# Four moves in the order of two attention and recurrence layers: bank emptying before the rotary exchange, Fourier products split, scores and output pieces swapped

## The chip, the cores and the metric

The kernel runs on one core of a Trainium2 chip. The time is the device time of one execution, in microseconds (us), from three runs before the change. The trace and the page of the profile come from one further execution.

Five engines work side by side and wait for each other by semaphores: TensorE (PE; its weight loads have a row of their own, PEld), VectorE (DVE), ScalarE (ACT), GpSimd (POOL) and SyncE (SP). TensorE writes its products into eight PSUM banks; ScalarE and VectorE empty them.

## What is computed

The reference is two blocks on 256 tokens of width 1024. The first (adaptive norm, attention, pooling, 32 experts) is left as it is. The second has two layers, and the change is in them:

```python
def second_block(x, positions, attn_norm_w, w_in, hgrn_lower_bounds, w_out, mlp_norm_w, w_up, w_down, final_norm_w):
    ...
    for layer in range(DEPTH_2):
        h = rms_norm_2(x, attn_norm_w[layer])
        proj = h @ w_in[layer]
        a_q, a_i, a_zf, a_zb, a_g, b_u, c_q, c_k, c_v = jnp.split(proj, SPLIT_POINTS, axis=-1)
        o_a = hgrn2_mixer(a_q, a_i, a_zf, a_zb, a_g, lb_all[layer]).astype(x.dtype)
        o_b = fourier_mixer(b_u).astype(x.dtype)
        o_c = dilated_attention_mixer(c_q, c_k, c_v, positions).astype(x.dtype)
        mixed = jnp.concatenate([o_a, o_b, o_c], axis=-1)
        x = x + mixed @ w_out[layer]
        h = rms_norm_2(x, mlp_norm_w[layer])
        x = x + jnp.square(jax.nn.relu(h @ w_up[layer])) @ w_down[layer]
    return rms_norm_2(x, final_norm_w)
```

`hgrn2_mixer` is a gated recurrence in two directions with 4 heads, `fourier_mixer` a 2-D Fourier transform of 256 columns, and `dilated_attention_mixer` an attention of 8 heads, with rotary positions on q and k. All data are float32.

## The kernel before

Every engine has one program, written out by hand in the order in which it runs: `pe_layer`, `dve_layer` and `act_layer` are called once for each layer (l = 0, 1). No scheduler moves anything. An engine that waits holds up all that stands behind it in its own program.

TensorE takes banks in a fixed rotation (`g.take`): all eight in turn, and in the attention part the first four only, while banks 4 to 7 hold the four output pieces. `take` waits until the bank's last content was read. `g.evac(e, key)` waits until that key's bank was read, `g.full` until it was written.

A layer runs on TensorE in this order. *Projections* of 256 columns each (L541, L553) fill banks "in" and "av". Between them stand the pieces of the recurrence:

- `pe_hgrn(l, dr, c)` for direction dr and half c. With c = 0 it first fills two **large** banks, "far" (L1125, L1131). Then it fills, for each of two token halves, two banks "lv" with 56 small products (L1146). VectorE prepares their inputs in `dve_decay` (last instruction L2278), and takes the results off in `dve_pairs` (L2295, L2297), which stands ahead of the decay of the next direction. The far banks are read by ScalarE in `act_far` (L1566, L1567, two of each). The last "lv" pair of direction 0 comes eight banks after the far pair, and so reuses its banks.
- `pe_hgrn_out` (L1171, L1173) multiplies what the pairs gave with the values. It waits for two copies by ScalarE (L1456, semaphore `placed`).
- the Fourier products "V" (L989) over channels, four of them, two for each 128 columns c, read by ScalarE at L1469; and four products each for "four" (L1004) over tokens, read at L1477.
- "os" (L993), the sum of squares of the recurrence's output.

The rotary exchange is `act_turn_halves`: ScalarE issues four DMAs (L1527) that swap halves of q (or k). VectorE multiplies and adds them (L2070, L2071, L2074); the third sum (`rot_ready` 3) admits the scores of head pairs 0 and 1, the fourth those of pairs 2 and 3.

The attention works on four head pairs c = 0 to 3 (heads 2c and 2c+1). `pe_layer_scores(c)` (L1186) makes two banks of scores; `pe_layer_turn(c)` (L1199) transposes the probabilities of its two heads; `pe_layer_mix(c)` (L1212) multiplies them with v; `pe_out_first` (L1231) is one of four output pieces of 16 matmul records, over the first half of `mix`, and depends on no head. VectorE's order for the heads is a loop:

```python
    for h in range(2, 8):
        dve_layer_score(e, g, l, h)
        if h > 2:
            dve_layer_prob(e, g, l, h - 1)
    dve_layer_prob(e, g, l, 7)
```

`dve_layer_score` reads a score bank (L2218) and finds the maxima (L2220); ScalarE exponentiates (L1536); `dve_layer_prob` divides by the sum (L2226, L2230) and raises `prob_ready`, for which the transposes of that head wait. After the attention comes the rest of the output (L1030), and the up and down projections, where TensorE works without a pause.

Of the kernel before, what the change touches and what calls it, by code (L numbers as in the profile page):

```python
# [10 lines left out]
P = 128  # L11
D = 1024
S = 256
KC = D // P
ST = S // P
# [516 lines left out]
def h_ready(e, g, n, k):  # L532
    e.wait_ge(g.s["h_shifted" if n < 2 else "h_scaled"], KC * n + k + 1)
# [410 lines left out]
def pe_layer(e, g, l):  # L944
    s = g.s
    n = 2 + 2 * l
    ready = lambda k: h_ready(e, g, n, k)
    raw = lambda which: lambda k: e.wait_ge(s["xw"], KC * (2 * l + which) + k + 1)

    def project(tile, oc):  # L950
        w = g.filled(e, layer_tile(l, tile))
        for jj in range(2):
            pe_chunk(e, g, ("in", l, oc + jj), w, jj, 256, KC, g.h, ready)
        g.owed += 1

    def tokens(tile, j):
        w = g.filled(e, layer_tile(l, tile))
        pe_tokens(e, g, ("av", l, j), w, g.h, ready)
        g.owed += 1

    for tile in range(2):
        w = g.filled(e, layer_tile(l, tile))
        for jj in range(2):
            pe_chunk(e, g, ("in", l, 4 + 2 * tile + jj), w, jj, 256, KC, g.xw, raw(0))
            if tile == jj == 0 and l:
                pe_norm_added(e, g, n)
            if tile == 0 and jj == 1 and l == 0:
                pe_norm_two(e, g)
        g.owed += 1
    project(2, 0)  # L970
    tokens(3, 0)
    project(4, 10)
    project(5, 12)
    pe_hgrn(e, g, l, 0, 0)
    pe_hgrn(e, g, l, 0, 1)
    project(6, 14)
    project(7, 16)
    project(8, 2)
    pe_hgrn(e, g, l, 1, 0)
    project(9, 8)  # L980
    pe_hgrn(e, g, l, 1, 1)
    tokens(10, 1)
    pe_hgrn_out(e, g, l)
    for c in range(2):
        for tt in range(ST):
            u = g.take(e, ("V", l, c, tt))
            e.wait_ge(s["late_in"], 16)
            g.evac(e, "in", l, 8 + c)
            g.last(u, e.matmul(u.ap[:, 0:S], g.uT[:, c, tt * P:(tt + 1) * P], g.c("dft_c"), start=True, stop=True))  # L989
    u = g.take(e, ("os", l))  # L990
    e.wait_ge(s["o_square"], 2 * l + 2)
    for c in range(2):
        ins = e.matmul(u.ap[:, c * S:(c + 1) * S], g.c("headones"), g.tmp4[:, c, :], start=True, stop=True)  # L993
    g.last(u, ins)
    pe_layer_scores(e, g, l, 0)
    tokens(11, 2)
    for c in range(2):
        u = g.take(e, ("four", l, c))
        e.wait_ge(s["late_in"], 16)
        for tt in range(ST):  # L1000
            g.evac(e, "V", l, c, tt)
        for n4 in range(4):
            part, tt = n4 // 2, n4 % 2
            ins = e.matmul(u.ap[:, 0:S], g.V[:, tt, c, part * P:(part + 1) * P], g.c("dft_t", (part * ST + tt) * S, S), start=n4 == 0, stop=n4 == 3)  # L1004
        g.last(u, ins)

    g.cycle, g.turn = range(4), 0
    out = []
    pe_layer_scores(e, g, l, 1)
    pe_layer_turn(e, g, l, 0)  # L1010
    pe_layer_scores(e, g, l, 2)
    pe_out_first(e, g, l, out)
    pe_layer_turn(e, g, l, 1)
    pe_layer_mix(e, g, l, 0)
    pe_layer_scores(e, g, l, 3)
    pe_out_first(e, g, l, out)
    pe_layer_turn(e, g, l, 2)
    pe_layer_mix(e, g, l, 1)
    pe_out_first(e, g, l, out)
    pe_layer_turn(e, g, l, 3)  # L1020
    pe_layer_mix(e, g, l, 2)
    pe_out_first(e, g, l, out)
    pe_layer_mix(e, g, l, 3)
    g.cycle, g.turn = range(8), 0
    for j in range(4):
        w = g.filled(e, layer_tile(l, 12 + j))
        for jj in range(2):
            for k in range(4, KC):
                g.evac(e, "m", l, k - 4)
                ins = e.matmul(out[j].ap[:, jj * S:(jj + 1) * S], w[:, k * 256 + jj * P:k * 256 + (jj + 1) * P], g.mix[:, k, :],  # L1030
                               start=False, stop=k == KC - 1, skip_group_check=True)
                if k < KC - 1:
                    g.hand_back(ins)
        g.last(out[j], ins)
        g.owed += 1

    for j in range(2):
        w = g.filled(e, layer_tile(l, 16 + j))
        for jj in range(2):
            oc = 2 * j + jj  # L1040
            pe_chunk(e, g, ("up", l, oc), w, jj, 256, KC, g.xw, raw(1))
            if oc == 0:
                pe_norm_added(e, g, n + 1)
        g.owed += 1
    for i in range(SEVENS):
        pe_seven(e, g, l, i)
    w = g.filled(e, layer_tile(l, 18 + SEVENS))
    e.wait_ge(s["hid_ready"], UPS * (l + 1))
    for jj in range(2):
        pe_chunk(e, g, ("down", l, jj), w, jj, 256, KC, g.hid[:, 24:32, :], lambda k: None)  # L1050
    g.owed += 1
# [102 lines left out]
def pe_hgrn_out(e, g, l):  # L1154
    for dr in range(2):
        for j in range(2):
            g.evac(e, "far", l, dr, j)
    e.wait_ge(g.s["far_out"], 4 * (l + 1))
    e.wait_ge(g.s["placed"], 2 * (l + 1))
    g.evac(e, "av", l, 0, 1)  # L1160
    for c in range(2):
        u = g.take(e, ("o", l, c))
        for tt in range(ST):
            for far in range(2):
                for j in range(2):
                    lo, hd = DH * j, 2 * c + j
                    v = slice(hd * DH, (hd + 1) * DH)
                    q = u.ap[lo:lo + DH, tt * P:(tt + 1) * P]
                    if far:
                        al = 4 * (1 - tt) + 2 * j + c  # L1170
                        ins = e.matmul(q, g.av[:, 1 - tt, v], g.AL[:, al * P:(al + 1) * P], start=False, stop=True)  # L1171
                    else:
                        ins = e.matmul(q, g.av[:, tt, v], g.AT[:, hd, tt * P:(tt + 1) * P], start=True, stop=False)  # L1173
                    if tt == far == 1 and j == 0:
                        ins.then_inc(g.s["o_half"], 1)
        g.last(u, ins)


def pe_layer_scores(e, g, l, c):

    us = [g.take(e, ("s", l, 2 * c + j)) for j in range(2)]
    e.wait_ge(g.s["rot_ready"], 4 * l + 3 + c // 2)
    for qt in range(ST):
        for j in range(2):
            lo = DH * j
            ins = e.matmul(us[j].ap[:, qt * S:(qt + 1) * S], g.cq[lo:lo + DH, c, qt * P:(qt + 1) * P], g.ck[lo:lo + DH, c, :],  # L1186
                           start=True, stop=True)
            if qt == 1:
                g.last(us[j], ins)


def pe_layer_turn(e, g, l, c):
    for j in range(2):
        h = 2 * c + j
        u = g.take(e, ("t", l, h))
        e.wait_ge(g.s["prob_ready"], 8 * l + h + 1)
        for kt in range(ST):
            for qt in range(ST):
                ins = e.transpose(u.ap[:, (2 * kt + qt) * P:(2 * kt + qt + 1) * P], g.prob[h % 4][:, qt * S + kt * P:qt * S + (kt + 1) * P],  # L1199
                                  g.c("ident"))  # L1200
        g.last(u, ins)


def pe_layer_mix(e, g, l, c):
    u = g.take(e, ("m", l, c))
    for j in range(2):
        g.evac(e, "t", l, 2 * c + j)
    g.evac(e, "av", l, 2, 1)
    for kt in range(ST):
        for j in range(2):  # L1210
            lo, h = DH * j, 2 * c + j
            ins = e.matmul(u.ap[lo:lo + DH, 0:S], g.cv[:, kt, h * DH:(h + 1) * DH], g.prob_t[h % 4][:, kt * S:(kt + 1) * S],  # L1212
                           start=kt == 0, stop=kt == 1)
            if kt == 1 and j == 0:
                ins.then_inc(g.s["mix_half"], 1)
    g.last(u, ins)


def pe_out_first(e, g, l, out):


    j = len(out)
    w = g.filled(e, layer_tile(l, 12 + j))
    u = g.take(e, ("lout", l, j), 4 + j)
    for jj in range(2):
        for k in range(4):
            if k < 2:
                e.wait_ge(g.s["hg_ready"], l + 1)
            else:
                g.evac(e, "four", l, k - 2)  # L1230
            e.matmul(u.ap[:, jj * S:(jj + 1) * S], w[:, k * 256 + jj * P:k * 256 + (jj + 1) * P], g.mix[:, k, :],  # L1231
                     start=k == jj == 0, stop=False, skip_group_check=True)
    out.append(u)
# [160 lines left out]
def act_layer(e, g, l):  # L1394
    s = g.s
# [40 lines left out]
            tokens(0)  # L1436
    for oc in range(10, 14):
        evict(oc)
    act_turn_halves(e, g, l, 0)
    act_far(e, g, l, 0)  # L1440
    for lv in range(NL):
        act_decay(e, g, l, 1, lv)
        if lv % 2 == 0:
# [1011 lines left out]
```

## Time and profile before

| what | value |
|---|---|
| median of 3 runs | 1407.7 us (1407.31 to 1408.53) |
| profiled execution, its time | 1408.37 us |
| profiled execution, its span | 1406.6 us, so 1.77 us lie around the span |
| TensorE busy | 1380.7 us |
| VectorE, ScalarE busy | 661.8 us, 264.2 us |
| granted TensorE clock, mean | 0.996 of full |

The span is from the first to the last instruction. Busy time of TensorE is the time in which a matmul is in flight; what is left of the span are its pauses. A row of the timeline gives in brackets how long the engine was idle before it and what ended that. "issue" is a pause for which the profile names no partner.

### The profile page before, as it was taken

Reading aid. Unit: us, or ns where it says so; the run is one execution under the profiler, and the core shown is the slowest. Engines: PE = TensorE matmul, PEld = TensorE weight load, DVE = VectorE, ACT = ScalarE, POOL = GpSimd, SP = SyncE. Lnnn points to the kernel's source line nnn. Section 1 sums busy time; section 2 is a strip of 40 time slices with the busy share of each in tenths; the row PEclk is TensorE's granted clock in tenths of the full one; section 3 lists DMA queues with packets and bytes.
Section 4 is the critical chain, followed back from the end, with each engine's and each line's share of the span. In section 5 each row is a group of like instructions: output and inputs, shape, how many; then the busy total and the mean of one; then the engine's idle time right before and its main releaser. Section 6 shows DMA issues by size and latency. Waiting matters only on the chain.

```text
span 1406.6 us, 22243 instructions
## 1 busy us (share of the span) xinstructions
PE 1380.7 (98%) x9402; PEld 1061.7 (75%) x9402; DVE 661.8 (47%) x1483; ACT 264.2 (19%) x565; POOL 4.0 (0%) x10
## 2 busy tenths in 40 slices
PE   9999999999999999999999999999999999999997
PEld 6888887454445544554488789999998878999997
DVE  2467554111111111111278837775445883777544
ACT  2234201100000000000243431220014343122000
POOL 0000000000000000000000000000000000000000
PEclk9999999999999999999999999999999999999999
DMA  9995656999999999999944224444544413444420
GB/s 392 354 398 197 265 215 274 422 422 420 420 420 422 420 421 420 423 421 421 418 166 132 83 101 171 178 161 169 181 150 150 151 61 124 171 158 179 165 76 31
DMA packets 51237, 362.95 MB, mean 258 GB/s; under 512 B 6064, under 2 KB 6384, under 8 KB 7872
## 3 DMA queue, kind: packets, MB, share of 16 engines
q1 hardware_dynamic: 48528, 353.39, 63.4%
q10 hardware_dynamic: 2032, 5.96, 1.4%
q0 software_dynamic: 576, 2.14, 0.4%
q8 instruction: 77, 1.26, 0.4%
q14 instruction: 24, 0.20, 0.0%
HBM read 358.31 MB, written 1.06 MB: 255 GB/s over the span
## 4 chain that ended last, share of the span: by engine, by line
PE 92%; DMA 2%; DVE 2%; ACT 1%; issue 1%; ACTq 0%; DVEq 0%; SPq 0%
PE bank L1094 26%; PE bank L839 22%; PE bank L541 19%; PE bank L553 4%; PE bank L827 4%; PE bank L849 4%; DMA ring<-in_weights 2%; PE bank L1231 2%; PE bank L658 2%; PE bank L1030 2%; PE bank L1186 1%; PE bank L1212 1%; PE bank L613 1%; PE bank L1146 1%; PE bank L1199 1%
## 5 line engine op out<-in xcount | busy, mean ns | idle before, releaser
L541 PE MATMUL bank<-h,ring 128*128 128x256 f32 x832 | 185.6, 383 | 0.8 <-issue 0.7
L541 PEld LDWEIGHTS bank<-h,ring 128*128 128x128 f32 x832 | 158.0, 191 | 23.8 <-issue 2.3
L839 PE MATMUL bank<-ring,x_s 128*64 128x512 f32 x768 | 167.8, 592 | 1.4 <-issue 0.9
L839 PEld LDWEIGHTS bank<-ring,x_s 128*64 128x64 f32 x768 | 56.1, 137 | 109.9 <-issue 109.9
L1094 PE MATMUL bank<-hid,ring 128*128 128x128 f32 x912 | 115.6, 275 | 0.0
L1094 PE MATMUL bank<-h,ring 128*128 128x128 f32 x896 | 113.8, 275 | 0.0
L1094 PEld LDWEIGHTS bank<-hid,ring 128*128 128x128 f32 x912 | 108.6, 192 | 0.0
L1094 PEld LDWEIGHTS bank<-h,ring 128*128 128x128 f32 x896 | 107.0, 192 | 0.1
L1936 DVE TENSOR_TENSOR act<-act,bank 128x512 f32<-128x512 f32 x16 | 11.0, 688 | 195.5 <-PE bank L839 195.5
L1094 PE MATMUL bank<-sq,ring 128*128 128x128 f32 x720 | 95.1, 275 | 0.0
L1094 PEld LDWEIGHTS bank<-sq,ring 128*128 128x128 f32 x720 | 87.6, 192 | 0.0
L839 PE MATMUL bank<-ring,a_s 128*64 128x512 f32 x384 | 85.0, 595 | 0.0
L553 PE MATMUL bank<-ring,h 128*128 128x256 f32 x320 | 71.2, 381 | 0.0
L1094 PE MATMUL bank<-ring 128*128 128x128 f32 x512 | 67.6, 275 | 0.0
L553 PEld LDWEIGHTS bank<-ring,h 128*128 128x128 f32 x320 | 60.2, 190 | 9.3 <-issue 1.3
L1919 DVE TENSOR_TENSOR x_s<-bank,mod 128x512 f32<-128x512 f32 x32 | 22.1, 692 | 95.7 <-PE bank L827 95.7
L839 PEld LDWEIGHTS bank<-ring,a_s 128*64 128x64 f32 x384 | 26.5, 137 | 49.4 <-issue 48.0
L1094 PEld LDWEIGHTS bank<-ring 128*128 128x128 f32 x512 | 62.3, 192 | 0.0
L849 PEld LDWEIGHTS bank<-put,gy 128*128 128x128 f32 x256 | 47.3, 190 | 19.8 <-issue 14.0
L827 PE MATMUL bank<-pick,h 128*128 128x128 f32 x512 | 61.4, 279 | 0.7 <-DVE pick L1911 0.7
L827 PEld LDWEIGHTS bank<-pick,h 128*128 128x128 f32 x512 | 59.9, 196 | 0.8 <-issue 0.8
L849 PE MATMUL bank<-put,gy 128*128 128x256 f32 x256 | 59.5, 385 | 1.0 <-DVE gy L1943 1.0
(353 smaller groups left out, 1734.7 us busy)
## 6 DMA issues: line engine op xcount, KB each, us to landing
ring<-in_weights SPq DMA_DIRECT2D x288, 1024.0 KB, 12.4
ringx<-in_weights SPq DMA_DIRECT2D x48, 1024.0 KB, 19.6
x<-in_x SPq DMA_DIRECT2D x1, 1024.0 KB, 5.1
pool_a<-in_cst ACTq DMA_DIRECT2D x1, 1024.0 KB, 6.2
bias<-bias_rows POOLq DMA_DIRECT2D x1, 1024.0 KB, 16.9
ring<-cq ACTq DMA_DIRECT2D x8, 128.0 KB
ring<-ck ACTq DMA_DIRECT2D x8, 128.0 KB, 2.4
out<-h ACTq DMA_DIRECT2D x2, 512.0 KB, 3.6
```

The source lines that it names most:

```text
L541: ins = e.matmul(u.ap[:, 0:S], w[:, k * width + j * P:k * width + (j + 1) * P], acts[:, k, :], start=k == 0, stop=k == kc - 1)
L553: ins = e.matmul(u.ap[:, 0:256], acts[:, k, tt * P:(tt + 1) * P], w[:, k * 256:(k + 1) * 256], start=k == 0, stop=k == KC - 1)
L613: ins = e.matmul(u.ap[32 * q:32 * q + 32, 0:256], g.spread[:, k, :], w[:, k * 256:(k + 1) * 256], start=m == 0, stop=m == 1)
L658: ins = e.matmul(u.ap[:, 0:S], w[:, k * 256 + jj * P:k * 256 + (jj + 1) * P], g.h[:, k, :], start=k == 0, stop=k == KC - 1)
L827: ins = e.matmul(g.bank[bank + k // 4][:, (k % 4) * P:(k % 4 + 1) * P], g.h_tok[:, tt, k * P:(k + 1) * P], g.pick[:, tt * P:(tt + 1) * P], ...
L839: ins = e.matmul(g.bank[bank][ex * SLOTS:(ex + 1) * SLOTS, :], stat(m)[:, ex * SLOTS:(ex + 1) * SLOTS], pair[ex][:, m * 512:(m + 1) * 512] ...
L849: ins = e.matmul(g.bank[4 + oc // 2][:, (oc % 2) * S:(oc % 2 + 1) * S], gy[:, oc * P:(oc + 1) * P], put[:, :], start=p == oc % 2 == 0, sto ...
L1030: ins = e.matmul(out[j].ap[:, jj * S:(jj + 1) * S], w[:, k * 256 + jj * P:k * 256 + (jj + 1) * P], g.mix[:, k, :], start=False, stop=k == ...
L1094: ins = e.matmul(u.ap[:, at * P:(at + 1) * P], a[:, k, :], act[:, k, :], start=k == 0 and (of == 1 or (b == 0 and first)), stop=k == 3 and ...
L1146: ins = e.matmul(us[j].ap[HB * b:HB * b + HB, lv * HB:(lv + 1) * HB], k, q, start=True, stop=True)
L1231: e.matmul(u.ap[:, jj * S:(jj + 1) * S], w[:, k * 256 + jj * P:k * 256 + (jj + 1) * P], g.mix[:, k, :], start=k == jj == 0, stop=False, sk ...
L1919: e.tensor_tensor(g.x_s[:, 512 * half:512 * half + 512].rearrange("p (k t) -> p k t", k=4), g.bank[bank + half][:, :].rearrange("p (k t) - ...
```

## The change

Three parts of a layer's order are written otherwise; no instruction is added or removed. `pe_channels` is a new function with the body of the old loop, for one c.

```diff
@@ -980,13 +980,9 @@
     project(9, 8)
     pe_hgrn(e, g, l, 1, 1)
     tokens(10, 1)
+    pe_channels(e, g, l, 0)
     pe_hgrn_out(e, g, l)
-    for c in range(2):
-        for tt in range(ST):
-            u = g.take(e, ("V", l, c, tt))
-            e.wait_ge(s["late_in"], 16)
-            g.evac(e, "in", l, 8 + c)
-            g.last(u, e.matmul(u.ap[:, 0:S], g.uT[:, c, tt * P:(tt + 1) * P], g.c("dft_c"), start=True, stop=True))
+    pe_channels(e, g, l, 1)
     u = g.take(e, ("os", l))
     e.wait_ge(s["o_square"], 2 * l + 2)
     for c in range(2):
@@ -1008,12 +1004,12 @@
     out = []
     pe_layer_scores(e, g, l, 1)
     pe_layer_turn(e, g, l, 0)
+    pe_out_first(e, g, l, out)
     pe_layer_scores(e, g, l, 2)
-    pe_out_first(e, g, l, out)
     pe_layer_turn(e, g, l, 1)
     pe_layer_mix(e, g, l, 0)
+    pe_out_first(e, g, l, out)
     pe_layer_scores(e, g, l, 3)
-    pe_out_first(e, g, l, out)
     pe_layer_turn(e, g, l, 2)
     pe_layer_mix(e, g, l, 1)
     pe_out_first(e, g, l, out)
...
@@ -1436,8 +1441,8 @@
             tokens(0)
     for oc in range(10, 14):
         evict(oc)
+    act_far(e, g, l, 0)
     act_turn_halves(e, g, l, 0)
-    act_far(e, g, l, 0)
```

The line numbers shift by a few. TensorE in the attention of the first layer, before: L1199 is a turn, L1186 scores, L1231 an output piece, L1212 a mix.

```order
L1199 MATMUL bank<-cst,hm 128x128 [waits prob_ready,bank_free_2]
...
L1199 MATMUL bank<-cst,hm 128x128 [waits prob_ready,bank_free_3]
...
L1186 MATMUL bank<-ck,cq 128x256 [waits rot_ready,bank_free_1,bank_free_0]
L1186 MATMUL bank<-ck,cq 128x256 x3
L1231 MATMUL bank<-mixed,ring 128x256 [waits hg_ready,bank_free_4,slot_filled_4]
...
L1231 MATMUL bank<-mixed,ring 128x256 [waits bank_free_6]
...
L1199 MATMUL bank<-cst,hm 128x128 [waits prob_ready,bank_free_2]
...
L1199 MATMUL bank<-cst,hm 128x128 [waits prob_ready,bank_free_3]
...
L1212 MATMUL bank<-hm,cv 64x256 [waits bank_free_3,bank_free_5,bank_free_2,bank_free_0]
```

The same place in the changed kernel (turn L1204, scores L1191, output piece L1236, mix L1217):

```order
L1204 MATMUL bank<-cst,hm 128x128 [waits prob_ready,bank_free_2]
...
L1204 MATMUL bank<-cst,hm 128x128 [waits prob_ready,bank_free_3]
...
L1236 MATMUL bank<-mixed,ring 128x256 [waits hg_ready,bank_free_4,slot_filled_4]
...
L1236 MATMUL bank<-mixed,ring 128x256 [waits bank_free_6]
...
L1191 MATMUL bank<-ck,cq 128x256 [waits rot_ready,bank_free_1,bank_free_0]
L1191 MATMUL bank<-ck,cq 128x256 x3
L1204 MATMUL bank<-cst,hm 128x128 [waits prob_ready,bank_free_2]
...
L1204 MATMUL bank<-cst,hm 128x128 [waits prob_ready,bank_free_3]
...
L1217 MATMUL bank<-hm,cv 64x256 [waits bank_free_3,bank_free_5,bank_free_2,bank_free_0]
```

The output piece and the scores of pair 2 have changed places, so that the turn of pair 1 stands right behind the scores of pair 2. Output piece 1 and the scores of pair 3, further down, change in the same way. The banks stay the same.

TensorE at the chunk outputs of the first layer, before (L1173 waits for `placed`, L989 are the Fourier products):

```order
L1173 MATMUL bank<-sq_106,av 64x128 [waits far_out,placed,bank_free_6,bank_free_0,bank_free_5,bank_free_3]
...
L1171 MATMUL bank<-hal,av 64x128 x2
...
L1173 MATMUL bank<-sq_106,av 64x128 [waits bank_free_4]
...
L989 MATMUL bank<-cst,uT 128x256 [waits bank_free_3,late_in,bank_free_5]
L989 MATMUL bank<-cst,uT 128x256 [waits bank_free_3,late_in,bank_free_6]
L989 MATMUL bank<-cst,uT 128x256 [waits bank_free_4,late_in,bank_free_7]
L989 MATMUL bank<-cst,uT 128x256 [waits bank_free_4,late_in,bank_free_0]
```

The same in the changed kernel (L1169 waits for `placed`, L1181 are the Fourier products):

```order
L1181 MATMUL bank<-cst,uT 128x256 [waits bank_free_3,late_in]
L1181 MATMUL bank<-cst,uT 128x256 [waits bank_free_3,late_in,bank_free_4]
L1169 MATMUL bank<-sq_106,av 64x128 [waits far_out,placed,bank_free_6,bank_free_0,bank_free_5]
...
L1167 MATMUL bank<-hal,av 64x128 x2
...
L1169 MATMUL bank<-sq_106,av 64x128 [waits bank_free_6]
...
L1181 MATMUL bank<-cst,uT 128x256 [waits bank_free_4,late_in,bank_free_7]
L1181 MATMUL bank<-cst,uT 128x256 [waits bank_free_4,late_in,bank_free_0]
```

Two of the four Fourier products now stand ahead of the wait for `placed`, in banks 3 and 4.

ScalarE behind the copies of q in the first layer, before: L1527 are the four DMA issues of the rotary exchange, L1566 and L1567 empty the far banks.

```order
L1418 COPY cq<-bank 128x256 [waits bank_full_4]
L1527 DMA ring<-cq 32x1024 [waits bank_free_3,bank_free_4,bank_free_2,bank_free_1]
L1527 DMA ring<-cq 32x1024 x3
L1566 COPY hal<-bank 128x256 [waits bank_full_5]
L1567 COPY sq_106<-bank 64x2x2x64
L1566 COPY hal<-bank 128x256 [waits bank_full_6]
L1567 COPY sq_106<-bank 64x2x2x64
L1558 ACTIVATE mixed<-mixed 128x512 [waits ex_in]
```

And in the changed kernel (L1532 are the issues, L1571 and L1572 empty the far banks):

```order
L1423 COPY cq<-bank 128x256 [waits bank_full_4]
L1571 COPY hal<-bank 128x256 [waits bank_full_5]
L1572 COPY sq_106<-bank 64x2x2x64
L1571 COPY hal<-bank 128x256 [waits bank_full_6]
L1572 COPY sq_106<-bank 64x2x2x64
L1532 DMA ring<-cq 32x1024 [waits bank_free_3,bank_free_4,bank_free_2,bank_free_1]
L1532 DMA ring<-cq 32x1024 x3
L1563 ACTIVATE mixed<-mixed 128x512 [waits ex_in]
```

The four copies stand ahead of the four issues.

## Rows read from the trace of the kernel before

**Rows 1.** The profile's page, busy time of TensorE, its share and instructions.

```profile
PE 1380.7 (98%) x9402; PEld 1061.7 (75%) x9402; DVE 661.8 (47%) x1483; ACT 264.2 (19%) x565; POOL 4.0 (0%) x10
```

**Rows 2.** TensorE's timeline, first layer, attention: start, duration, line, tiles, [idle before].

```profile
804.62 1.09 PE L1199 MATMUL bank<-cst,hm 128*128 128x128 f32 x8
806.84 1.13 PE L1186 MATMUL bank<-ck,cq 64*128 64x256 f32 x8 [1.12 <-issue]
807.90 3.72 PE L1231 MATMUL bank<-mixed,ring 128*128 128x256 f32 x16
811.46 1.04 PE L1199 MATMUL bank<-cst,hm 128*128 128x128 f32 x8
812.43 1.08 PE L1212 MATMUL bank<-hm,cv 128*64 128x256 f32 x8
813.44 1.13 PE L1186 MATMUL bank<-ck,cq 64*128 64x256 f32 x8
```

**Rows 3.** VectorE's timeline in the same stretch of the first layer.

```profile
802.25 0.69 DVE L2087 TENSOR_TENSOR mixed<-sg,gs 128x512 f32<-128x512 f32 x1
...
806.05 0.68 DVE L2218 SCALAR_TENSOR_TENSOR hm<-bank,cst 128x512 f32<-128x512 f32 x1
...
808.10 0.68 DVE L2218 SCALAR_TENSOR_TENSOR hm<-bank,cst 128x512 f32<-128x512 f32 x1
...
809.42 0.15 DVE L2226 RECIPROCAL small<-small 128x2 f32<-128x2 f32 x1
809.61 0.62 DVE L2230 TENSOR_SCALAR hm<-hm,small 128x256 f32<-128x256 f32 x2
...
814.68 0.69 DVE L2218 SCALAR_TENSOR_TENSOR hm<-bank,cst 128x512 f32<-128x512 f32 x1 [2.41 <-PE bank L1186]
```

**Rows 4.** ScalarE's timeline there: the second Fourier bank is emptied.

```profile
803.67 0.37 ACT L1477 COPY mixed<-bank 128x256 f32<-128x256 f32 x1 [1.36 <-PE bank L1004]
```

**Rows 5.** TensorE's timeline, blocks L1146 and L1125, both layers.

```profile
745.41 0.93 PE L1146 MATMUL bank<-hm 64*64 64x64 f32 x48 [0.70 <-ACT sq L1567]
...
767.65 0.71 PE L1125 MATMUL bank<-hm 64*128 64x128 f32 x8
...
1093.54 0.81 PE L1146 MATMUL bank<-hm 64*64 64x64 f32 x38 [0.70 <-ACT sq L1567]
1095.37 0.39 PE L1146 MATMUL bank<-hm 64*64 64x64 f32 x10 [1.03 <-issue]
...
1116.72 0.71 PE L1125 MATMUL bank<-hm 64*128 64x128 f32 x8
```

**Rows 6.** VectorE's timeline, last row of the second decay, both layers.

```profile
767.16 0.42 DVE L2278 TENSOR_TENSOR hm<-mixed,kk 128x256 f32<-128x256 f32 x1
...
1115.39 0.42 DVE L2278 TENSOR_TENSOR hm<-mixed,kk 128x256 f32<-128x256 f32 x1
```

**Rows 7.** ScalarE's timeline, second layer: rotary exchange issued, last large bank emptied.

```profile
1089.72 2.46 ACTq L1527 DMA_DIRECT2D ring<-cq  x4
...
1093.01 0.38 ACT L1567 COPY sq<-bank 64x256 f32<-64x256 f32 x1
```

**Rows 8.** DMA queues from 1093.00 to 1093.25 us: packets, MB, share of 16 engines.

```profile
q10 hardware_dynamic: 13, 0.05, 98.8%
q8 instruction: 1, 0.02, 23.6%
```

**Rows 9.** TensorE's timeline, first layer: chunk outputs, Fourier products, first scores.

```profile
787.24 0.44 PE L1173 MATMUL bank<-sq,av 128*64 128x128 f32 x4 [0.63 <-ACT sq L1456]
...
789.14 2.00 PE L989 MATMUL bank<-cst,uT 128*128 128x256 f32 x8
...
791.93 1.13 PE L1186 MATMUL bank<-ck,cq 64*128 64x256 f32 x8
```

**Rows 10.** ScalarE's copies into `AT` (first), VectorE's third rotary sum, first layer.

```profile
785.63 1.26 ACT L1456 COPY sq<-sq 64x512 f32<-64x512 f32 x2 [7.50 <-DVE sq L2063]
...
790.90 0.69 DVE L2074 TENSOR_TENSOR ck<-ck,ring 128x512 f32<-128x512 f32 x1
```

More of the change, by code:

```diff
@@ L1176, in pe_hgrn_out, with pe_channels @@
         g.last(u, ins)
+def pe_channels(e, g, l, c):
+    for tt in range(ST):
+        u = g.take(e, ("V", l, c, tt))
+        e.wait_ge(g.s["late_in"], 16)
+        g.evac(e, "in", l, 8 + c)
+        g.last(u, e.matmul(u.ap[:, 0:S], g.uT[:, c, tt * P:(tt + 1) * P], g.c("dft_c"), start=True, stop=True))
 def pe_layer_scores(e, g, l, c):
```

## The prediction

> **What bounds the kernel now.** I read the page first, for the share of TensorE. It is busy for 1380.7 us [rows 1] of a span of 1406.6, so a new order can gain no more than its 25.9 us of pauses, and any new pause is added in full, as nothing behind it waits for anything but TensorE. Then I read TensorE's timeline in both layers for the pauses at the three places that change. They are few: 1.12 us ahead of the scores of pair 2 [rows 2], 0.70 us ahead of the last L1146 block and, in the second layer, 1.03 us inside it [rows 5], and 0.63 us ahead of the chunk outputs [rows 9]. Last I read VectorE and ScalarE at the same moments, for what each pause waited for and what comes due right behind it. These rows decide the sum: a pause that is removed is worth only what lies between it and the next due time. The attention part has the same shape in both layers, so I work it out once and take it twice. All sums are made for the profiled execution (1408.37 us, its span and 1.77 us around it); it lies 0.67 us above the median of 1407.7, and I carry the difference to the median.
>
> **Attention, what is removed.** From the first turn (804.62) to the scores of pair 2 (806.84) pass 2.22 us [rows 2]. A turn with nothing in its way passes in 811.46 to 812.43, 0.97 us. So the pause costs 1.25 us at the pace of starts. The profile calls it "issue", but the scores need the two banks that VectorE is still reading: its second L2218 ends at 806.05 + 0.68 = 806.73 [rows 3] and the scores start at 806.84, 0.11 us later. In the new order output piece 0 stands here. What it needs is there: `hg_ready` at 802.25 + 0.69 = 802.94 [rows 3] and the second "four" bank at 803.67 + 0.37 = 804.04 [rows 4], against 805.59, when the turn is over. The piece passes in 807.90 to 811.46, 3.56 us [rows 2], longer than the pause. The 1.25 us go.
>
> **Attention, what is added.** The turn of pair 1 now stands right behind the scores of pair 2. Its second head, 3, needs `dve_layer_prob(3)`, and that stands in VectorE's loop behind `dve_layer_score(4)`, which needs the scores that TensorE has only just made. Before, the output piece lay over this round trip. Now it is bare. I work it out from the start S of the scores:
>
> - VectorE begins the score of the new pair at S + 1.24, as at 813.44 and 814.68, where it did wait for them [rows 2, 3].
> - From that to the division of the head before it pass 809.42 − 808.10 = 1.32 us, and the division ends 0.81 us later (809.61 + 0.62 − 809.42) [rows 3]. That is S + 3.37.
> - TensorE starts 0.11 us later, by the 806.73 and 806.84 above: S + 3.48.
> - TensorE itself is there after the scores (806.84 to 807.90, 1.06 us [rows 2]) and the transposes of the first head (half of 0.97, 0.49): S + 1.55.
>
> The new pause is 1.93 us, and it occurs twice in a layer, with scores 2 and scores 3. Behind the waiting transposes stand the mix, the next output piece and the next scores, so VectorE and ScalarE get everything later too, and the second pause is not filled by the first. The third and fourth turn have output pieces ahead of them as before. Sum for a layer: 2 × 1.93 − 1.25 = +2.61 us, for two +5.2 us. The least sure number is 0.11 us for waking TensorE. Behind ScalarE's copies into `AT`, which end at 785.63 + 1.26 = 786.89, TensorE started at 787.24, 0.35 us later [rows 9, 10]. With that in all four places the sum is 5.2 + 4 × 0.24 = +6.2 us. I take 0.11, as it is VectorE that wakes TensorE in both places.
>
> **The large banks.** ScalarE spends 2.46 us on four DMA issues ahead of the copies, and the last copy ends at 1093.01 + 0.38 = 1093.39 [rows 7]; the block starts at 1093.54 [rows 5]. TensorE has filled the far pair before the three L1146 blocks that precede this one, so copies that stand ahead of the issues start up to 2.46 us sooner, and the 0.70 us wait goes in both layers. What is due next is the next L1125, which needs VectorE's whole second decay. In the first layer the decay ends at 767.16 + 0.42 = 767.58 [rows 6] and TensorE is there at 767.65 [rows 5]. TensorE cannot come any earlier: worth 0. In the second it ends at 1115.39 + 0.42 = 1115.81 [rows 6], TensorE is there at 1116.72 [rows 5], and with 0.11 to wake it 0.80 us are to be had at most. VectorE's chain up to there has no gap that this edit shortens, as it still has the decay to do that stands behind the pairs.
>
> Whether the 0.80 are reached hangs on the 1.03 us inside the block [rows 5]. No engine released it. In the quarter microsecond from 1093.00 the instruction queue q8 began one packet, while the rotary exchange on q10 filled the DMA engines to 98.8% [rows 8]. I read the 1.03 us as instructions that had not yet arrived. Then they arrive at their own time, and TensorE, started earlier, waits longer there. The exchange now begins more than a microsecond later, which may let the packet through sooner. Bounds 0 and 0.80; I take 0.4 us, for the second layer alone. The later exchange itself costs nothing: the first layer's rotary sums end at 791.59 [rows 10], 46 us behind the block of 745.41 [rows 5].
>
> The Trainium skill ("Runtime: NRT & Kernel Launch", Instruction fetch mechanics) says that instructions are fetched in blocks of 256 and that crossing from one block to the next is mostly hidden. By that rule the 1.03 us would be no fetch, and the 0.80 us would be gained whole, which makes the sum 0.4 us smaller. The trace speaks against it with the 1.03 us beside the q8 packet.
>
> **The Fourier products.** Two of the four (half of the 2.00 us of eight records [rows 9]) now run while TensorE waited 0.63 us for ScalarE. They cover the wait. But behind them comes the first scores at 791.93 [rows 9], which need the third rotary sum; VectorE has it at 790.90 + 0.69 = 791.59 [rows 10]. With 0.11 us to wake, 791.70: of the 0.63 us no more than 0.23 remain, and with 0.35 to wake nothing. I take 0.1 for each layer, 0.2 us in all, bounds 0 and 0.46. VectorE's own chain is not shortened by this edit.
>
> **Sum.** +5.2 − 0.4 − 0.2 = +4.6 us: 1408.37 becomes 1413.0, the median 1407.7 becomes 1412.3. By the bounds: least 5.2 − 0.80 − 0.46 = +3.9, most +6.2, so 1411.6 to 1413.9.
>
> **Rivals.** 0.2% of the time, 2.8 us, is about what a measurement of this kernel can tell from no change.
>
> - *Both early edits pay in full, the attention costs what I say.* The pauses at the large banks (2 × 0.70 + 1.03) and at the chunk outputs (2 × 0.63) are 3.7 us. Then 5.2 − 3.7 = +1.5 us, 1409.2. It needs VectorE to be off the path in between; the two pairs 767.58 / 767.65 and 791.59 / 791.93 speak against it.
> - *Faster: the round trip is not bare.* If the probabilities of head 3 were there by S + 1.55, the two swaps would only remove 1.25 us each, and with my 0.6 the kernel would gain 3.1 us: 1404.6. It decides at a round trip of 1.55 us against my 3.48; VectorE's two scans and division alone take 2.13 of it, so little speaks for it. It would need the loop to stand otherwise.
> - *The cost is larger.* The attention at its upper bound, and one more instruction gap of 1.03 us in each layer, since blocks of instructions now end in other places against the waits: 6.2 + 2.1 = +8.3, less what the early edits give (0.6): 1415.4. For it speaks the 1.03 us itself; against it that no other such gap shows in the stretches I read.
> - *Attention as forecast, the early edits worth nothing:* inside my range, 1412.9.
>
> **How the numbers follow.** My forecast has 72 in 100, the full early gains 12, the larger cost 11, the faster case 5. The predicted time is that of the likeliest, 1412.3. Its own range is 1411.6 to 1413.9. The range over all cases goes down to 1410.0, which takes in partial gains of the first rival, and up to 1414.6, half way to the larger cost. Faster by over 0.2% (below 1404.9): 0.04. Within 0.2% (to 1410.5): 0.14. Slower: 0.82.
>
> **What would show it.** In the new trace the scores of pair 2 have no pause ahead of them, and the transposes of heads 3 and 5 each start after about 1.9 us of pause, released by L2230's counterpart on VectorE; the stretch from the first turn to the rest of the output (L1030) is 2.6 us longer in each layer. If these pauses are under 1 us, the step "round trip bare" is wrong. ScalarE's last far copy ends ahead of the last L1146 block, and that block starts without a wait; the next L1125 starts at the end of VectorE's decay in both layers. If it starts later in the second, the instructions were late. Ahead of the chunk outputs there is no pause, and there is one of about half a microsecond ahead of the first scores. The prediction is wrong as a whole if the time lies at or below 1410, which would mean that the early edits moved VectorE's chain too.

## The result, and the profile after

The changed kernel takes 1420.09 us (six runs, 1415.14 to 1421.34) where the kernel before takes 1408.05 (six runs, 1407.21 to 1408.53): a ratio of 1.0081, interval 1.0067 to 1.0095. It is slower, as forecast, but by 12.0 us and not by 4.6. Two executions of one later kernel, `swap_half_filled`, took 1451.86 and 1797.84 us at a mean granted clock of 0.944 and 0.752 and are left out of its times. The profiled execution of the changed kernel took 1419.98 us:

```profile
span 1418.1 us, 22243 instructions
...
PE 1386.2 (98%) x9402; PEld 1063.5 (75%) x9402; DVE 661.9 (47%) x1483; ACT 263.3 (19%) x565; POOL 4.1 (0%) x10
```

The span has grown by 11.5 us, TensorE's busy time by 5.5 [rows 1], though it has the same 9402 matmul records (a float32 product leaves two). So a good part of the loss is not a pause: the same work took longer. TensorE's timeline in the attention of the first layer answers to [rows 2] (turn L1204, scores L1191, output piece L1236, mix L1217, rest of the output L1026):

```profile
804.37 1.09 PE L1204 MATMUL bank<-cst,hm 128*128 128x128 f32 x8
805.30 3.62 PE L1236 MATMUL bank<-mixed,ring 128*128 128x256 f32 x16
808.85 1.14 PE L1191 MATMUL bank<-ck,cq 64*128 64x256 f32 x8
809.91 0.66 PE L1204 MATMUL bank<-cst,hm 128*128 128x128 f32 x4
812.36 0.63 PE L1204 MATMUL bank<-cst,hm 128*128 128x128 f32 x4 [1.79 <-DVE hm L2235]
812.92 1.82 PE L1217 MATMUL bank<-hm,cv 128*64 128x256 f32 x8
814.67 4.63 PE L1236 MATMUL bank<-mixed,ring 128*128 128x256 f32 x16
819.23 1.14 PE L1191 MATMUL bank<-ck,cq 64*128 64x256 f32 x8
...
822.74 0.62 PE L1204 MATMUL bank<-cst,hm 128*128 128x128 f32 x4 [1.79 <-DVE hm L2235]
823.30 1.95 PE L1217 MATMUL bank<-hm,cv 128*64 128x256 f32 x8
825.17 4.50 PE L1236 MATMUL bank<-mixed,ring 128*128 128x256 f32 x16
829.51 1.04 PE L1204 MATMUL bank<-cst,hm 128*128 128x128 f32 x8
...
836.15 4.15 PE L1026 MATMUL bank<-mixed,ring 128*128 128x256 f32 x18
```

The pause ahead of the scores is gone. The turn of pair 1 stops after its first head, and the second starts at 812.36 after 1.79 us, released by VectorE's L2235 (before: L2230), and the same at 822.74. But look at what follows. The first mix passes in 812.92 to 814.67, 1.75 us, where it took 1.01 before (812.43 to 813.44 [rows 2]); the output piece takes 4.56 us (814.67 to 819.23) and not 3.56. The windows show why (the columns are the stretch, its length, and the busy time and, in brackets, the instructions of PE, PEld, DVE, ACT and POOL; then PEclk, the granted clock, 1.00 being full, the DMA share and GB/s):

```profile
812.90:814.70 1.80, 1.80 (x10) 0.72 (x9) 1.32 (x4) 1.13 (x5) 0.00 (x0) 0.56 0.00 0
814.70:819.20 4.50, 4.50 (x18) 3.57 (x16) 0.00 (x0) 1.19 (x3) 0.00 (x0) 0.80 0.00 0
...
823.30:825.20 1.90, 1.90 (x10) 0.78 (x9) 1.43 (x5) 1.25 (x5) 0.00 (x0) 0.52 0.04 9
825.20:829.50 4.30, 4.30 (x18) 3.67 (x17) 0.66 (x3) 1.07 (x3) 0.00 (x0) 0.82 0.00 2
829.50:836.10 6.60, 6.60 (x41) 4.73 (x39) 0.00 (x0) 1.45 (x3) 0.00 (x0) 1.00 0.00 0
```

Right behind each of these pauses the granted clock is near half, the lower of its levels (1.2 GHz); over the output piece it averages 0.80 and 0.82, and in the last window it is back at the full 2.4 GHz. From the first turn to the rest of the output pass 836.15 − 804.37 = 31.78 us; before it was

```profile
804.62:830.25 25.63, 24.51 (x147) 18.89 (x145) 12.11 (x30) 12.29 (x36) 0.00 (x0) 1.00 0.00 1
```

The 6.15 us more are two pauses at the pace of starts, 809.91 to 812.36 less the 0.49 of one head, 1.96 us each, less the 1.25 removed: 2.67 us. The other 3.5 us are the work behind them at the lower clock: 0.74 and 1.00 behind the first pause, 0.86 and 0.78 behind the second (mix 823.30 to 825.17, output piece 825.17 to 829.51), and 0.07 for each second head. The second layer is alike, 1191.26 − 1159.53 = 31.73 us where 25.62 passed, so both layers together lose 12.3 us: 5.3 of pauses and 7.0 behind them.

That TensorE's busy time grew by 5.5 us and not by 7.0 comes for the most part from a place that the change does not touch. In the first block stand three pauses of 0.70, 0.99 and 0.73 us within some five microseconds, in both profiled executions. Behind them the clock fell in that of the kernel before and not in that of the changed kernel. The first row and window are of the kernel before, the second ones of the changed kernel:

```profile
107.12 8.83 PE L541 MATMUL bank<-h,ring 128*128 128x256 f32 x32 [0.73 <-issue]
107.12:115.79 8.67, 8.67 (x32) 7.34 (x33) 5.83 (x20) 4.38 (x12) 0.00 (x0) 0.80 0.09 35
...
107.09 7.15 PE L541 MATMUL bank<-h,ring 128*128 128x256 f32 x32 [0.73 <-issue]
107.09:114.07 6.98, 6.98 (x33) 6.17 (x33) 4.25 (x17) 2.71 (x10) 0.00 (x0) 1.00 0.11 43
```

The same 32 records take 1.7 us more where the clock averages 0.80. VectorE's side of the pause, answering to [rows 3]:

```profile
810.08 0.69 DVE L2223 SCALAR_TENSOR_TENSOR hm<-bank,cst 128x512 f32<-128x512 f32 x1 [2.16 <-PE bank L1191]
...
811.60 0.62 DVE L2235 TENSOR_SCALAR hm<-hm,small 128x256 f32<-128x256 f32 x2
```

The score waits 2.16 us for TensorE, starts 1.23 us after the scores (808.85), and the division ends at 812.22, 0.14 us before the transposes start. This is the round trip as I had it.

The early edits, in the block of [rows 5] and at the places of [rows 9]:

```profile
746.39 0.34 PE L1142 MATMUL bank<-aq,kk 64*64 64x64 f32 x7 [1.29 <-issue]
746.67 3.50 PE L541 MATMUL bank<-h,ring 128*128 128x256 f32 x15
```

```profile
1101.39 0.39 PE L1142 MATMUL bank<-hm 64*64 64x64 f32 x10 [2.07 <-issue]
```

```profile
787.34 0.44 PE L1169 MATMUL bank<-sq,av 128*64 128x128 f32 x4
...
791.67 1.14 PE L1191 MATMUL bank<-ck,cq 64*128 64x256 f32 x8 [0.21 <-DVE ck L2079]
```

ScalarE's wait of 0.70 us is gone, and one pause ("issue") of 1.29 us stands in its place in the first layer, of 2.07 us in the second, where 1.03 stood. The projection starts at 746.67. The next L1121 (before: L1125) starts at 767.59 and 1122.74 us, 0.39 and 1.02 us behind the end of VectorE's decay (767.20 and 1121.72). Ahead of the chunk outputs (787.34) is no pause, and there is one of 0.21 ahead of the first scores.

### The profile page after: what moved, and what is told of

It is laid out like the page before. It is cut to its first block, busy times and chain, and to the rows that moved or that the text cites. A ratio compares the mean times of both kernels' runs of the same rounds, so it can differ in the third digit from the quotient of the medians.

```text
span 1418.1 us, 22243 instructions
## 1 busy us (share of the span) xinstructions
PE 1386.2 (98%) x9402; PEld 1063.5 (75%) x9402; DVE 661.9 (47%) x1483; ACT 263.3 (19%) x565; POOL 4.1 (0%) x10
## 3 DMA queue, kind: packets, MB, share of 16 engines
q8 instruction: 77, 1.26, 0.3%
## 4 chain that ended last, share of the span: by engine, by line
PE 91%; DVE 4%; DMA 2%; issue 1%; ACT 1%; DVEq 0%; SPq 0%; ACTq 0%
PE bank L1090 26%; PE bank L839 22%; PE bank L541 18%; PE bank L553 4%; PE bank L827 4%; PE bank L849 4%; DMA ring<-in_weights 2%; PE bank L1236 2%; PE bank L658 2%; PE bank L1026 2%; PE bank L1142 1%; PE bank L1217 1%; PE bank L1191 1%; PE bank L613 1%; PE bank L1000 0%
## 5 line engine op out<-in xcount | busy, mean ns | idle before, releaser
L541 PE MATMUL bank<-h,ring 128*128 128x256 f32 x832 | 183.9, 381 | 1.3 <-issue 1.2
L541 PEld LDWEIGHTS bank<-h,ring 128*128 128x128 f32 x832 | 157.3, 190 | 23.4 <-issue 2.7
```

What stands on the lines that cost most here:

```text
L541: ins = e.matmul(u.ap[:, 0:S], w[:, k * width + j * P:k * width + (j + 1) * P], acts[:, k, :], start=k == 0, stop=k == kc - 1)
```

## Experiments

Each is compared with the kernel before on the same chip. There the kernel before had medians of 1407.46, 1409.23, 1408.94 and 1408.88 us, and its executions spread from 1405.9 to 1410.9. The ratio compares the executions of one round with each other, and each difference in us below is worked out from the ratio (0.1% is 1.4 us), not from the medians.

**The exchange alone, and the early edits alone.** `swap_only` has only this:

```diff
     pe_layer_turn(e, g, l, 0)
+    pe_out_first(e, g, l, out)
     pe_layer_scores(e, g, l, 2)
-    pe_out_first(e, g, l, out)
     pe_layer_turn(e, g, l, 1)
     pe_layer_mix(e, g, l, 0)
+    pe_out_first(e, g, l, out)
     pe_layer_scores(e, g, l, 3)
-    pe_out_first(e, g, l, out)
```

> Only the scores and output pieces change places. Theory 1 (the pauses ahead of heads 3 and 5 cost 2.7 us a layer, and TensorE's clock falls to half behind each of them, another 3.5 us a layer): +12.3 us, 1420.3 against 1408.0, with the granted clock near 0.5 right behind each 1.8 us pause. Theory 2 (the early edits have a part in the loss): clearly less, +5 to +9 us.

Measured: 1420.49 us, ratio 1.0087 (1.0070 to 1.0103), +12.2 us. The exchange alone makes a loss of the same size as the whole change. `early_only` has the other two parts of the diff and not this one.

> Only ScalarE's copies ahead of the rotary exchange and the Fourier split; the attention as before. Theory 1: what these edits remove is due again right behind, so -0.2 to -1.0 us, and no loss. Theory 2 (they cost something): +3 to +7 us.

Measured: 1409.29 us, ratio 1.0005 (0.9993 to 1.0017). That is no loss of the size of theory 2. A gain isn't shown either; the interval reaches from −1.0 to +2.4 us. The trace shows what can eat the gain. It is of an execution of 1410.26 us, and in its second layer stand:

```profile
1096.13 0.39 PE L1142 MATMUL bank<-hm 64*64 64x64 f32 x10 [1.79 <-issue]
```

```profile
1098.00:1100.00 2.00, 2.00 (x6) 1.58 (x5) 1.97 (x4) 0.00 (x0) 0.00 (x0) 0.50 0.69 229
```

Where I had hoped for a gain of 0.4 us stands a pause of 1.79 us, and behind it the clock is at half: 6 matmul records in 2 us, where the kernel before has 11. In the first layer of the same execution the pause is 1.64 us and the clock stays full.

**Pause or clock.** Is it TensorE's standing still that slows the work behind it, or VectorE and ScalarE reading banks beside it? `swap_filled` is the changed kernel with work in the pause:

```diff
         u = g.take(e, ("t", l, h))
+        if j and c in (1, 2):
+            for i in range(4):
+                e.matmul(u.ap[:, 0:S], g.c("ident"), g.c("dft_t", 0, S), start=True, stop=True)
         e.wait_ge(g.s["prob_ready"], 8 * l + h + 1)
```

> The changed kernel, with four products of 128x256 that nobody reads put into the bank of the second head ahead of its wait, in the turns of pairs 1 and 2: 1.73 us of work inside a pause of 1.96 us at the pace of starts. Extra work is done, the wait for the head stays. Theory 1 (the clock falls because TensorE stands still): the clock stays at 1.0 and the mix and output piece behind take 1.01 and 3.56 us as before the change; the time is before + 5.3 - 0.9, about 1412.5, some 7 us faster than the changed kernel. Theory 2 (mix and output piece are slow because VectorE and ScalarE read banks beside them): no faster than the changed kernel, 1420.

Measured: 1412.63 us, ratio 1.0034 (1.0022 to 1.0046), +4.8 us. It does more work than the changed kernel and is about 7 us faster. The trace is of an execution of 1416.37 us, one of the slower ones, as the clock fell elsewhere in it (behind a pause of 1.72 us in the small-product block of the first layer). L1203 are the unread products, L1207, L1220 and L1239 turn, mix and output piece:

```profile
813.51 1.89 PE L1203 MATMUL bank<-cst 128*128 128x256 f32 x8
815.38 0.66 PE L1207 MATMUL bank<-cst,hm 128*128 128x128 f32 x4
815.96 1.08 PE L1220 MATMUL bank<-hm,cv 128*64 128x256 f32 x8
816.98 3.72 PE L1239 MATMUL bank<-mixed,ring 128*128 128x256 f32 x16
820.63 1.14 PE L1191 MATMUL bank<-ck,cq 64*128 64x256 f32 x8
```

```profile
815.96:816.98 1.02, 1.02 (x10) 0.49 (x9) 0.98 (x3) 0.30 (x1) 0.00 (x0) 1.00 0.00 0
816.98:820.63 3.65, 3.65 (x19) 2.96 (x17) 0.38 (x2) 2.01 (x7) 0.00 (x0) 1.00 0.00 0
```

The second head still starts 2.36 us behind the first (813.02 to 815.38), so nearly all of the round trip is still there (2.45 us in the changed kernel). The mix takes 1.02 us and the output piece 3.65, at full clock, and so in all four places of the two layers. The stretch from the first turn to the rest of the output takes 28.39 us (807.47 to 835.86), 2.8 more than before; the prediction has 2.6.

`swap_half_filled` has two such products in place of four.

> The changed kernel with two unread products in the waits of heads 3 and 5 in place of four, so that TensorE stands still for about 0.9 us there and not 1.79. Theory 1 (a pause as long as 1.8 us lets the clock fall; the 1.12 us ahead of scores 2 in the kernel before did not): clock 1.0 behind it, time as with four products, 1412 to 1413. Theory 2 (any pause at this place with little work around it does it): the falls stay, 1416 to 1420.

```profile
815.47 0.66 PE L1207 MATMUL bank<-cst,hm 128*128 128x128 f32 x4 [0.84 <-DVE hm L2238]
```

```profile
816.00:820.00 4.00, 4.00 (x24) 3.08 (x23) 1.38 (x5) 2.32 (x7) 0.00 (x0) 1.00 0.00 0
```

With 0.84 us left to stand still the clock holds, in all four places. Two executions count, 1414.63 and 1416.32 us, too few for an interval. The rows bear theory 1 out, the time does not confirm it: the profiled execution, 1416.32, had a fall elsewhere, behind a pause of 2.00 us in the small-product block of the first layer.

**One exchange.** `swap_one` moves only output piece 0 ahead of scores 2:

```diff
     pe_layer_turn(e, g, l, 0)
+    pe_out_first(e, g, l, out)
     pe_layer_scores(e, g, l, 2)
-    pe_out_first(e, g, l, out)
     pe_layer_turn(e, g, l, 1)
```

> The kernel before with only the first of the two exchanges: output piece 0 ahead of scores 2; scores 3 stay ahead of output piece 1. Theory 1: one round trip of 1.96 us at the pace of starts is bare and one fall of the clock follows, the 1.25 us ahead of scores 2 go: +0.7 + 1.75 = +2.5 us a layer, +5 us in all. Theory 2 (the loss of the exchanges is joint, one alone is free or gains): -2.5 to +1 us.

Measured: 1413.41 us, ratio 1.0033 (1.0020 to 1.0045), +4.7 us. One exchange costs by itself, so the loss is not a joint effect of the two. But they do not cost the same. In the trace the stretch is longer by 2.6 us in the first layer and 2.7 in the second, where both exchanges cost 6.1: each has its pause of 1.96 us and its fall, and the 1.25 us that the change removes are credited to the first alone.

```profile
811.89 0.63 PE L1199 MATMUL bank<-cst,hm 128*128 128x128 f32 x4 [1.80 <-DVE hm L2230]
```

```profile
814.00:816.00 2.00, 1.63 (x8) 1.15 (x8) 0.00 (x0) 1.42 (x5) 0.00 (x0) 0.51 0.00 0
816.00:820.00 4.00, 4.00 (x21) 3.21 (x20) 3.35 (x8) 1.09 (x4) 0.00 (x0) 1.00 0.00 0
```

**The cause of the round trip.** `swap_dve` is the changed kernel with another order on VectorE:

```diff
     for h in range(2, 8):
         dve_layer_score(e, g, l, h)
-        if h > 2:
-            dve_layer_prob(e, g, l, h - 1)
-    dve_layer_prob(e, g, l, 7)
+        if h % 2:
+            dve_layer_prob(e, g, l, h - 1)
+            dve_layer_prob(e, g, l, h)
```

> The changed kernel, with VectorE dividing heads 2 and 3 ahead of score 4, and heads 4 and 5 ahead of score 6. Theory 1 (the pause is the round trip through score h+1 that VectorE's loop puts ahead of the division): the pauses ahead of heads 3 and 5 go, and with them the clock's falls; what is left is the gain, 2 x 1.25 for the pause ahead of scores 2 and some 0.6 of the early edits: 1404.9. Theory 2 (the division is late for another reason, as ScalarE's exponentials): pauses of 1 us or more stay.

Measured: 1405.75 us, ratio 0.9986 (0.9976 to 0.9996), faster than the kernel before. The first turn, the turn of pair 1 and the rest of the output:

```profile
804.54 1.09 PE L1204 MATMUL bank<-cst,hm 128*128 128x128 f32 x8
...
810.08 1.10 PE L1204 MATMUL bank<-cst,hm 128*128 128x128 f32 x8
...
829.08 11.28 PE L1026 MATMUL bank<-mixed,ring 128*128 128x256 f32 x51
```

```profile
808.53 0.17 DVE L2231 RECIPROCAL small<-small 128x2 f32<-128x2 f32 x1 [0.44 <-ACT hm L1541]
808.73 0.62 DVE L2235 TENSOR_SCALAR hm<-hm,small 128x256 f32<-128x256 f32 x2
810.25 0.69 DVE L2223 SCALAR_TENSOR_TENSOR hm<-bank,cst 128x512 f32<-128x512 f32 x1 [0.90 <-PE bank L1191]
```

Head 3 is divided at 808.73 to 809.35, ahead of score 4 at 810.25, and the turn at 810.08 runs through. The stretch takes 24.54 us where 25.63 passed, 1.1 less. `swap_dve_only` is this exchange and this order without the early edits.

> The exchange of scores and output pieces with VectorE's divisions moved ahead of the next scores, ScalarE and the Fourier products as before. Theory 1 (the early edits give little or nothing, as their pause is due again): the 1.1 us a layer that the attention lost by its pause are gained, 1405.2 to 1405.8 where before is 1407.5. Theory 2 (the early edits gave a good part of the 1.7 us): half of that gain or less, 1406.5 or more.

Measured: 1406.87 us, ratio 0.9986 (0.9976 to 0.9995), the same ratio as with them, and each is known to 0.1%. Theory 1 held, also in that no gain of the early edits shows.

**The pause in the small-product block.** I had read it as the wait for the next block of instructions. `early_shifted` is `early_only` with products that nobody reads in the routing part, 128 instructions:

```diff
         ins = e.matmul(u.ap[:, 0:512], g.xs[:, 0, 0:P], g.xs[:, 0:2, :], start=True, stop=True)
+    for i in range(32):
+        ins = e.matmul(u.ap[0:64, 0:64], g.xs[:, 0, 0:64], g.xs[:, 0, 0:64], start=True, stop=True)
     g.last(u, ins)
```

> Only the two early edits, and 32 products of 64x64 that nobody reads, 128 instructions of TensorE, put into the routing part some 500 us ahead. Theory 1 (the pause in the last small-product block is the wait for the next block of 256 instructions): it now comes 64 product records earlier, in the third small-product block of each layer, and leaves the fourth. Theory 2 (it is a wait for an engine or a bank): it stays where it was, in the fourth block ahead of record 39 or 50.

```profile
745.89 0.80 PE L1144 MATMUL bank<-hm 64*64 64x64 f32 x40
747.61 0.28 PE L1144 MATMUL bank<-hm 64*64 64x64 f32 x4 [0.92 <-issue]
```

One execution, 1408.67 us. The four blocks begin at 744.26, 745.03, 745.89 and 747.86; the pause has moved into the third, some 64 product records earlier, 500 us after the extra instructions were issued. The profile names no engine or bank for it there. So what sets the place is the count of instructions ahead of it. In the second layer too the pause now lies in the third block. It is also shorter, 0.92 and 1.26 us (1.64 and 1.79 in `early_only`).

**Each early edit alone.** `far_only` has only ScalarE's copies ahead of the exchange, `fourier_only` only the split.

> The kernel before with ScalarE's four copies ahead of the rotary exchange, nothing else. Theory 1 (the next block of instructions decides): the 0.70 us wait goes and the pause ahead of record 39 or 50 of the block grows to 1.3 to 2.1 us, so that the projection behind starts as late as before against the first L1125, 5.5 to 6.3 us; the stretch from the first to the second L1125 is not shorter than 26.7 us in the first layer; time within 1 us of before, or 1 to 2 us above it where the clock falls behind the longer pause. Theory 2 (the bank decides): the stretch of the second layer is 0.8 us shorter and the time 1 us lower.

Measured: 1411.30 us, ratio 1.0013 (1.0004 to 1.0023): this edit makes the kernel slower, by 1.8 us.

```profile
745.85 0.34 PE L1146 MATMUL bank<-aq,kk 64*64 64x64 f32 x7 [1.55 <-issue]
```

The 0.70 us wait is gone, the pause is 1.55 us (and 1.79 in the second layer), and the projection starts (at 746.12 in the first layer) 6.36 and 6.59 us after the first L1125 (739.76 and 1088.43), where 5.80 and 6.75 passed before. I had expected 5.5 to 6.3. In all the traces without the 128 extra instructions this distance is 5.80 to 6.75 us with the copies behind the exchange and 6.00 to 6.86 with the copies ahead of it, so to put them ahead buys nothing. The profiled execution, 1408.41, shows no fall of the clock; of the ten executions the five above 1411 us have a mean clock of 0.993 to 0.995, the one below 1408 has 0.997. The rows give a loss of 0.4 us (first to second L1125: 27.27 and 27.51 us, before 26.72 and 27.66). That the rest of the 1.8 us is the clock, behind the longer pause, is likely by these means and not shown by a trace.

> The kernel before with the Fourier products split, nothing else. Theory 1 (VectorE's third rotary sum is due right behind): no pause at the chunk outputs, one of 0.21 us ahead of the first scores, and the stretch from the second L1125 to the first scores is 0.2 us shorter in each layer (24.08 where 24.28 passed): -0.4 us in all. Theory 2 (the 0.63 us are gained whole): 23.6 us in each stretch, -1.3 us.

Measured: 1407.30 us, ratio 0.9992 (0.9983 to 1.0002), too close to 1 to be told apart from it. The rows settle it:

```profile
787.02 0.44 PE L1169 MATMUL bank<-sq,av 128*64 128x128 f32 x4
...
791.35 1.13 PE L1191 MATMUL bank<-ck,cq 64*128 64x256 f32 x8 [0.21 <-DVE ck L2079]
```

The stretch from the second L1125 (767.27) to the first scores is 24.08 us, where 24.28 passed (767.65 to 791.93 [rows 5, 9]): 0.2 us a layer, as theory 1 has it.

**Better than both.** `swap_dve_shifted` is `swap_dve` with the 128 extra instructions, `swap_dve_fourier` is `swap_dve` with ScalarE's copies back behind the exchange.

> The changed kernel with VectorE's divisions moved and the 128 extra instructions in the routing part. Theory 1 (shorter pauses at the instruction blocks, and so no fall of the clock behind them): the pauses of 1.2 to 2.1 us in the last small-product block become about 0.9 to 1.3 us in the third, and the kernel is 0.5 to 1 us faster than without the shift, ratio to before 0.9980. Theory 2 (the place of the instruction blocks does not matter to the time, or the extra products cost what it brings): ratio 0.9986 as without it.

> The changed kernel with VectorE's divisions moved, and ScalarE's copies back behind the rotary exchange, since alone they made the kernel slower (1.0013). Theory 1 (the copies ahead of the exchange join two short pauses into one of 1.2 to 2.1 us, behind which the clock falls in some executions): faster than with them (0.9986), 0.9970 to 0.9980. Theory 2 (they are neutral here): 0.9986.

Measured: 1406.04 us, ratio 0.9979 (0.9970 to 0.9988), and 1406.10 us, ratio 0.9982 (0.9973 to 0.9991). Both are faster than the kernel before and than the changed one. Among themselves and against 0.9986 they can't be told apart, so the expected order of the three is not shown. With the shift all eleven executions lie in 1405.7 to 1407.5 us.

## Why the prediction was wrong in size

- **The step that failed** stands in its first paragraph: "any new pause is added in full". It is added with more than itself. The sum had +5.2 us for the attention; it was +12.3, of which the pauses are 2 × 2.67 = 5.3, and 7.0 are work behind them at the lower clock. The term was not mis-sized but missing: none of the rivals had the clock. The page before had a mean clock of 0.996 and I took that for full, without asking what a longer pause than the longest of these stretches (1.12 us) would do to it. The trace of the kernel before already had the term: L541 at 107.12 us takes 8.83 us for 32 records behind three short pauses, while the same row of the changed kernel takes 7.15 at full clock. `swap_filled` shows it: the same wait with TensorE at work costs 4.8 us, and its 1412.6 us is within the predicted range; with TensorE at rest it costs 12.
- **The round trip was right.** Forecast 1.93 us a pause, measured 1.96; forecast 2.61 us a layer for the exchange, measured 2.67. VectorE's latency (1.24 against 1.23), its two scans and divisions, and the wake of 0.11 us (measured 0.14) all held, and `swap_dve` shows that the order in VectorE's loop is the cause.
- **The large banks:** that the 1.03 us are instructions that have not arrived fits `early_shifted`, where the pause moves with the count of instructions. In the first layer nothing is to be had, as forecast; 0.3 us were even lost (767.59 − 740.57 = 27.02 us between the two L1125, before 26.72). Wrong that the second gains 0.4 us: from the first L1125 to the second passed 1122.74 − 1094.97 = 27.77 us, where 27.66 passed before (1089.06 to 1116.72, the latter in [rows 5]). The prediction did say that TensorE, started earlier, waits longer there, and 0 was its lower bound. What it left out is that two short pauses so become one long one, and what the clock can do behind that. The exchange began later, but by 0.9 us in the second layer (issues 1.56 us after the first L1121 at 1094.97, before 0.66 after L1125), not by more than a microsecond: the DMA issues do not wait for the copies to end. In the first layer,

```profile
741.93 0.37 ACT L1571 COPY hal<-bank 128x256 f32<-128x256 f32 x1 [0.88 <-PE bank L1127]
742.11 0.61 ACTq L1532 DMA_DIRECT2D ring<-cq  x1
742.20 0.37 ACT L1572 COPY sq<-bank 64x256 f32<-64x256 f32 x1
```

  they began at 742.11, in among the copies. The instruction packet did not gain by it: in the second layer it begins in the quarter microsecond from 1099.00, 4.0 us after the first L1121, beside the exchange at 102.3% of the DMA engines (before: from 1093.00, 3.9 us after, at 98.8% [rows 8]).
- **The rule of the Trainium skill** ("Runtime: NRT & Kernel Launch", Instruction fetch mechanics) that crossing between blocks is mostly hidden does not hold in these small-product blocks, if the pauses are such crossings, as `early_shifted` says: 0.9 to 2.1 us in every trace with the copies ahead of the exchange. With the copies behind it 0.2 to 1.0 us stand beside the 0.70 us wait for ScalarE.
- **The Fourier products:** forecast 0.1 us a layer, bounds 0 and 0.23; measured 0.20. The pause ahead of the first scores was forecast at half a microsecond and is 0.21.
- **The rival "the cost is larger"** had the right direction and the wrong mechanism. It gave 1415.4.

## What to carry to other kernels

On a kernel that is bound by TensorE, price a new pause by two terms: the pause, and the work behind it at the lower clock. Here each pause of 1.8 us in the attention drew 1.6 to 1.9 us more after it, while single pauses of 0.84 and 1.12 us there drew none. Short ones are not safe where several stand close together: the three in the first block (0.70, 0.99, 0.73 us) drew 1.7 us in the profiled execution of the kernel before. Ahead of an exchange on one engine look in the program of the other for what stands between the request and the answer: the same exchange was +12 us with VectorE's old order and −2 us with the new. And before one of two short pauses is removed, look whether the other grows by as much and they join into a long one.

## What the runs showed that I had not expected

- A pause of about 1.8 us ahead of the second head was followed by the lower clock at all four places of the changed kernel, all four of `swap_only` and both of `swap_one`: the mix right behind took 1.42 to 1.98 us by its row where it takes 1.08 at full clock. In the small-product blocks pauses of that length were followed by it in some (1.79 in `early_only`, 1.72 in `swap_filled`, 2.00 in `swap_half_filled`) and not in others (2.07 in the changed kernel, 1.85 and 1.86 in the second layers of `swap_filled` and `swap_half_filled`, 1.79 in `far_only`). The three pauses of the first block, the same to 0.01 us, were followed by it in the profiled execution of the kernel before and not in that of the changed kernel. The length of the pause alone does not decide; what does, stays open. What stands around it differs (128x128 transposes in the one place, 64x64 products in the other), and no run separates that.
- The executions of one and the same kernel differ, in part by this. The kernel before, on one chip, took 1405.9 to 1407.9 us with a mean clock of 0.996 to 0.998, and 1408.6 to 1410.2 with 0.994 or 0.995. The fall in the first block stands in ten of the fourteen traces and costs 1.0 to 2.2 us in them. It is not the only cause: on another chip an execution of 1409.2 us had 0.998.
- The place of the instruction blocks matters. 128 instructions that do nothing, 500 us ahead, moved the pause of `early_only` and made it shorter (1.64 to 0.92 us in the first layer, 1.79 to 1.26 in the second).
